# One plain column pair fewer and one more by Strassen's scheme in four feed-forward layers, with the activation sums asked for twice as densely

## The chip, the cores and the metric

The kernel runs on one core of one Trainium2 chip. The metric is the device time of one execution in microseconds (us), lower is better. A difference under 0.2% is about what a measurement of this kernel can't tell from none.

## What is computed

The reference is two transformer blocks one after the other, on 512 tokens of width 1024, in float32. The first has two layers, each with a feed-forward layer ("ffn1"), a mixer of three branches, and a second feed-forward layer ("ffn2"); the second has a mixer of four branches and a feed-forward layer with a convolution. The four feed-forward layers of the first block are those of this change:

```python
def swiglu(x, w_gu, w_down):
    gate, up = jnp.split(x @ w_gu, 2, axis=-1)
    return (jax.nn.silu(gate) * up) @ w_down
...
    h = layer_norm(DEEPNORM_ALPHA * x + 0.5 * swiglu(x, ffn1_w_gu, ffn1_w_down), ln_g[0], ln_b[0])
    ...
    return layer_norm(DEEPNORM_ALPHA * h + 0.5 * swiglu(h, ffn2_w_gu, ffn2_w_down), ln_g[2], ln_b[2])
```

`w_gu` is 1024 x 5632. Its first 2816 columns make the gate, the others what is multiplied by it: 22 column tiles of 128 each (FT = 22). A gate tile with the tile of the same number of the other half is a column pair, so each of the four layers has 22 pairs.

## The kernel before, in words

**Numbers.** Every float32 operand of a large product is split in a rounded high part and a rest ("hi" and "lo", type fp32r), and a product is hi*hi + hi*lo + lo*hi: three matmuls. Activations lie transposed, 128 features by 512 tokens to a page.

**Plain products.** `product` makes one column tile, 128 x 512: 8 blocks of 128 x 128 weights, 3 matmuls of 512 columns each (`block_matmuls`, L2490, L2491, L2499). Four blocks in the order of use make a slab of weights, 128 x 512, 256 KB. A slab is loaded by SyncE (`load_slab`, L3806), rounded by ScalarE (`round_slab`, L2813) and its rest is made by VectorE (`rest_slab`, L3235); the first matmul of the slab waits for that rest. There are 14 raw buffers and 9 for rounded parts. How far ahead the steps of a slab stand in each engine's queue is set by `place`, which is called once a block:

```python
        if j == 0:
            self.loaded(min(s - 1 + LOADED, self.limit - 1))
            self.rested(s)
        if j == 1:
            self.rounded(min(s + AHEAD, self.limit - 1))
        if j == 3:
            self.rested(min(s + AHEAD - 1, self.limit - 1))
```

With AHEAD = 4, the rest of slab s + 3 is put on VectorE's queue at the last block of slab s. The limit is the end of the plain products at the head.

**Pairs by Strassen's scheme.** A pair can also be made by 7 products of half size (`paired`, `pair_product`): each is 4 blocks of 3 matmuls with 256 columns (`pair_matmuls`, L2525, L2527, L2528), 84 matmuls in all. They come in the order q1, q5, q4 of the pair before, q6, q3, q2, q7. For a pair the weights have to be combined first (`prepare`, run step by step): 5 loads by SyncE (L3810), two of them added to by accumulating DMAs that GpSimd issues (L3799), two sums on VectorE (L3241 `sum_second`, L3247 `sum_fourth`), rounding on ScalarE (L2824 for one unit, L2822 for two), and rests on VectorE (L3256 for one unit, L3253 for two). q1 needs the rest of the single unit, q5 the first wide rest, q6 the second. The activations have to be combined too, once a layer: `sums_of` makes for each of 4 page pairs four half-page differences on VectorE (L3264, L3265, L3268, L3271; called T here), two rounded parts on ScalarE (L2829, L2832) and two rests on VectorE (L3277 twice; called S here). It is a generator that gives way between its parts:

```python
            self.sums_made(k, self.R[kt].f, self.R[4 + kt].f, self.Rt[kt], self.Rt[4 + kt], a, b)
            self.Rt[kt] = self.Rt[4 + kt] = k["t4"]
            for _ in range(4):
                yield
            k.will(scalar="ha hb", vector="la lb")
            self.sums_split(k, scale, a, b, ha, hb)
```

with four more `yield` at the end, so a page pair takes 8 steps and all take 32, and a 33rd ends it.

**The head of such a layer** (`ffn`). The first ALONE = 6 pairs are made plain. In three layers the first three pairs are made while the normalised activations come in (`Pace.begin`); in the first layer, which starts the kernel, it is two. Then one pair after the other is made by the loop in `ffn`: ahead of each column tile `taken_in` takes one finished pair in if there is one (ScalarE silu L2925, VectorE product L3454, ScalarE rounding L2928, VectorE rest L3457), and then 9 rounds per tile (8 blocks, and one that ends it) each emit a block and `self.bg.steps(1)`, one step of the sums. In the last plain pair the rounds also call `head.step(until=6)`: the six first steps of `prepare` for the first pair by Strassen's scheme. Each engine's instructions stand in its queue in the order in which Python calls them. `Pace` has a model of time that orders the background work in the mixers; in this loop it plays no part, as the sums alone are in its queue.

After the head come the pairs ALONE to FIRST - 1 by Strassen's scheme, then the first part of the down projection over FIRST = 11 tiles, then the other 11 pairs by Strassen's scheme, and the rest of the down projection.

Of the kernel before, what the change touches and what calls it, by code (L numbers as in the profile page):

```python
# [30 lines left out]
T5_MAX_DIST = 128  # L31

SLAB = 4
NSLAB = 1120 - 4 * 64
NPAIR = 64
NRAW = 14
NHI = 9
LOADED = 7
# [6 lines left out]
CONST_PARTS = 4  # L45
NGAIN = 48
UNIT = SLAB * P
ALONE = 6
FIRST = 11
QUARTERS = ("a11", "a21", "a22", "a12")  # L50

# [432 lines left out]
class Order:  # L484
# [29 lines left out]
    def __init__(self, memory):  # L514
# [8 lines left out]
        self.pair_order = []  # L523
        self.slab, self.multiplied, self.limit = {}, 0, NSLAB
        self.next_block = self.next_raw = self.next_round = self.next_rest = 0
# [19 lines left out]
    def until(self, blocks):  # L545

        self.limit = min(-(-(self.next_block + blocks) // SLAB), NSLAB)

    def loaded(self, s):
        while self.next_raw <= min(s, NSLAB - 1):  # L550
            unit = self.raws.take()
            self.slab[self.next_raw] = [unit, None]
            self.landing(unit)
            self.load_slab(self.next_raw, unit)
            self.next_raw += 1

    def rounded(self, s):
        while self.next_round <= min(s, NSLAB - 1):
            self.loaded(self.next_round)
            raw, hi = self.slab[self.next_round] = [self.slab[self.next_round][0], self.his.take()]  # L560
            self.round_slab(self.next_round, raw, hi)
            self.next_round += 1

    def rested(self, s):
        while self.next_rest <= min(s, NSLAB - 1):
            self.rounded(self.next_rest)
            self.rest_slab(self.next_rest, *self.slab[self.next_rest])
            self.next_rest += 1
# [494 lines left out]
    def ffn(self, source, X, up, down, scale, early, after, scaled=None, mem=None):  # L1063
        H = Operand(FIRST)
        pairs = [m for j in range(ALONE) for m in (j, FT + j)]
        self.until(len(pairs) * DT)
        if early:
            first = self.bg.got(self.bg.begin(source, X, [early.product(up, m) for m in pairs[:2]],
                                              [self.product(up, m, X) for m in pairs[2:6]], early.made))
        else:  # L1070
            first = self.bg.got(self.bg.begin(source, X, [], [self.product(up, m, X) for m in pairs[:4]], lead=2))
        open_pairs = [first[i:i + 2] for i in range(0, len(first), 2)]

        def taken_in():
            gate, lift = open_pairs.pop(0)
            s = self.pages.take()
            k = self.marks("ffn").will(scalar="silu", vector="times")
            h, l = self.pages.take(), self.pages.take()
            k.will(scalar="round", vector="rest")
            self.ffn_act(k, gate, lift, s, h, l)  # L1080
            self.banks.give(gate, k["silu"])
            self.banks.give(lift, k["times"])
            H.join((h, l, k["rest"]))
            self.pages.give(s, k["rest"])

        if scaled:
            self.bg.get(scaled)
        sums = self.bg.add(self.sums_of(X, 1.0 / ALPHA))
        head = self.pair(up, ALONE, FT + ALONE)
        for m in range(len(open_pairs), ALONE):  # L1090
            made = []
            for n in (m, FT + m):
                if open_pairs:
                    taken_in()
                w = Later(self.product(up, n, X))
                while not w.done:
                    self.bg.tell(w)
                    self.bg.steps(1)
                    if m == ALONE - 1 and not w.done and (n > FT or self.next_block % DT in (2, 5)):
                        head.step(until=6)  # L1100
                made.append(w.value)
            open_pairs.append(made)
        self.bg.get(sums)
        while open_pairs:
            taken_in()

        def ahead(blocks):
            self.until(blocks)
            s = self.next_block // SLAB
            self.loaded(s + 1)  # L1110
            yield
            self.loaded(s + 2)
# [3 lines that stand above are left out]
            self.loaded(s + 3)  # L1116
            self.rested(s + 1)
            yield
            self.loaded(s + 4)
            self.rested(s + 2)  # L1120

        head.step(until=6)
        follow = Later(self.product(down, 0, H))
        self.paired(up, range(ALONE, FIRST), X, H, head, ahead(FIRST * DT), follow)
        part, H = H, Operand(FT - FIRST)
        head = self.pair(up, FIRST, FT + FIRST)
        left = FIRST * DT
        for m in range(DT):
            w = Later(self.product(down, m, part)) if m else follow
            while not w.done:  # L1130
                self.bg.tell(w)
                left -= 1
                if left in (24, 20, 12, 9, 6, 3):
                    head.step()
            k = self.marks("norm").will(vector="sum")
            self.add_up(k, w.value, m, scale)
            self.Rt[m] = k["sum"]
            self.banks.give(w.value, k["sum"])
        self.drop(part, w.value.full)
        follow = Later(self.product(down, 0, H, k0=FIRST))  # L1140
        self.paired(up, range(FIRST, FT), X, H, head, ahead(NSLAB * SLAB), follow)
        self.drop(X, (self.lanes["pair"].tensor, self.lanes["pair"].raised[0]))
        return self.update(down, H, scale, Spread(self, after, after.count == 2), k0=FIRST, beside=mem, begun=follow)
# [900 lines left out]
    def run(self):  # L2044
# [7 lines left out]
        assert SLAB * (NSLAB - 1) < self.next_block <= SLAB * NSLAB, self.next_block  # L2052
        assert len(self.pair_order) == NPAIR, len(self.pair_order)

# [1922 lines left out]
```

## Time and profile before

| | us |
|---|---|
| median of 3 runs | 3561.03 |
| lowest and highest | 3560.19, 3562.94 |
| the profiled execution: span from first to last instruction | 3557.1 |
| TensorE busy with matmuls | 3502.0 |
| VectorE busy | 2226.9 |
| ScalarE busy | 1679.6 |

The median is 3.9 us over the span of the profiled execution, which is what lies around the span. Busy times of TensorE count overlapping, pipelined matmuls once, and their ends are modelled, so starts are what to go by: the time from one matmul's start to the next one's. An idle time in brackets stands ahead of the instruction that ended it, with what it had waited for.

### The profile page before, as it was taken

How to read it: one execution, taken by the hardware profiler on the slowest of the kernel's cores; microseconds unless marked ns; L12 is line 12 of the kernel's file. 1: busy time of each engine (PE TensorE's matmuls, PEld its weight loads, DVE VectorE, ACT ScalarE, POOL GpSimd, SP SyncE). 2: the span in 40 equal slices, each digit the busy share in tenths (PEclk: the TensorE clock that was granted, in tenths of full speed). 3: DMA queues.
4: the chain of work that ended last, by engine and by line, in shares of the span. 5: the costliest groups of instructions: out<-in, count | busy, mean ns of one | idle time of the engine just before them, and what ended most of it. 6: DMA issues, size and time to landing. Idle time of an engine off the chain costs nothing.

```text
span 3557.1 us, 49763 instructions
## 1 busy us (share of the span) xinstructions
PE 3502.0 (98%) x19256; PEld 2932.2 (82%) x19256; DVE 2226.9 (63%) x4229; ACT 1679.6 (47%) x3243; POOL 111.3 (3%) x132
## 2 busy tenths in 40 slices
PE   9999999999999999999999999999999999999999
PEld 7898878877888987998888877888977677788887
DVE  5566656556775667566665566765676786666643
ACT  5354455554353545454555543553455443444432
POOL 0010000000000100010000000001000000000000
PEclk9999999999999999999999999999999999999999
DMA  5474331112335743574221112255522222233332
GB/s 154 131 175 143 116 95 48 45 47 72 90 105 138 173 122 98 140 172 125 83 66 47 47 60 91 93 134 151 152 79 86 69 66 84 77 94 93 95 95 86
DMA packets 198276, 358.86 MB, mean 101 GB/s; under 512 B 22102, under 2 KB 26359, under 8 KB 198040
## 3 DMA queue, kind: packets, MB, share of 16 engines
q1 hardware_dynamic: 178840, 321.32, 29.8%
q0 software_dynamic: 18432, 33.56, 5.6%
q8 instruction: 153, 2.51, 0.3%
q10 hardware_dynamic: 768, 0.79, 0.1%
q14 instruction: 83, 0.68, 0.1%
HBM read 350.60 MB, written 4.72 MB: 100 GB/s over the span
## 4 chain that ended last, share of the span: by engine, by line
PE 93%; DVE 4%; ACT 2%; issue 1%; DMA 0%; DVEq 0%; ACTq 0%
PE bank L2490 21%; PE bank L2499 21%; PE bank L2491 21%; PE bank L2525 6%; PE bank L2527 6%; PE bank L2528 6%; PE bank L2478 2%; PE bank L2473 1%; PE bank L2568 1%; PE bank L2661 1%; PE bank L2671 1%; PE bank L2536 1%; PE bank L2759 1%; PE bank L2588 1%; DVE w_lo L3235 0%
## 5 line engine op out<-in xcount | busy, mean ns | idle before, releaser
L2490 PE MATMUL bank<-page_r,w_hi 128*128 128x512 f32 (+1 forms) x3446 | 1383.4, 401 | 21.9 <-DVE w_lo L3235 14.7
L2499 PE MATMUL bank<-page_r,w_lo 128*128 128x512 f32 (+1 forms) x3446 | 1359.7, 395 | 0.0
L2491 PE MATMUL bank<-page_r,w_hi 128*128 128x512 f32 (+1 forms) x3446 | 1349.8, 392 | 0.0
L2490 PEld LDWEIGHTS bank<-page_r,w_hi 128*128 128x128 f32 x3446 | 650.0, 189 | 182.5 <-DVE w_lo L3235 18.8
L2813 ACT ACTIVATE w_hi<-raw 128x512 fp32r<-128x512 f32 x864 | 532.8, 626 | 558.3 <-PE bank L2499 550.1
L2499 PEld LDWEIGHTS bank<-page_r,w_lo 128*128 128x128 f32 x3446 | 649.2, 188 | 145.7
L2491 PEld LDWEIGHTS bank<-page_r,w_hi 128*128 128x128 f32 x3446 | 649.9, 189 | 141.6 <-issue 3.6
L3235 DVE TENSOR_TENSOR w_lo<-raw,w_hi 128x512 fp32r<-128x512 f32 x864 | 574.9, 686 | 150.2 <-ACT w_hi L2813 149.8
L2525 PE MATMUL bank<-page_r,w_hi 128*128 128x256 f32 x1792 | 503.7, 281 | 2.5 <-DVE w_lo L3253 2.5
L2528 PE MATMUL bank<-page_r,w_lo 128*128 128x256 f32 x1792 | 503.4, 281 | 0.0
L2527 PE MATMUL bank<-page_r,w_hi 128*128 128x256 f32 x1792 | 503.4, 281 | 0.0
L2525 PEld LDWEIGHTS bank<-page_r,w_hi 128*128 128x128 f32 x1792 | 337.7, 188 | 3.9 <-ACT page_f L2842 3.2
L2527 PEld LDWEIGHTS bank<-page_r,w_hi 128*128 128x128 f32 x1792 | 337.6, 188 | 0.7
L2528 PEld LDWEIGHTS bank<-page_r,w_lo 128*128 128x128 f32 x1792 | 337.7, 188 | 0.0
L3325 DVE SCALAR_TENSOR_TENSOR page_f<-bank,page_f 128x512 f32<-128x512 f32 x96 | 66.3, 691 | 261.6 <-PE bank L2499 260.6
L3253 DVE TENSOR_TENSOR w_lo<-raw,w_hi 128x1024 fp32r<-128x1024 f32 x192 | 228.8, 1220 | 0.0
L2822 ACT ACTIVATE w_hi<-raw 128x1024 fp32r<-128x1024 f32 x192 | 202.2, 1056 | 43.0 <-DVE raw L3247 21.3
L3799 POOL DMA_DIRECT2D raw<-pairs x128 | 111.1, 892 | 2425.4 <-DMA raw<-pairs 2424.0
L2842 ACT ACTIVATE page_f<-bank 128x256 f32<-128x256 f32 x128 | 49.2, 384 | 208.5 <-PE bank L2528 208.5
L2885 ACT ACTIVATE page_f<-page_f 128x512 f32<-128x512 f32 (+1 forms) x81 | 48.4, 604 | 130.8 <-DVE page_f L3325 112.6
L3776 DVE SCALAR_TENSOR_TENSOR page_f<-bank,par,page_f 128x511 f32<-128x511 f32 x88 | 65.5, 749 | 60.7 <-ACT page_f L3195 59.1
L2982 ACT ACTIVATE page_f<-bank 128x256 f32<-128x256 f32 (+3 forms) x129 | 45.4, 392 | 104.8 <-PE bank L2478 104.5
(322 smaller groups left out, 3462.9 us busy)
## 6 DMA issues: line engine op xcount, KB each, us to landing
raw<-weights SPq DMA_DIRECT2D x864, 256.0 KB, 2.7
raw<-pairs SPq DMA_DIRECT2D x320, 256.0 KB, 3.3
raw<-pairs POOLq DMA_DIRECT2D x128, 256.0 KB, 5.8
page_f<-x_t SPq DMA_DIRECT2D x8, 256.0 KB, 5.2
bias_rows<-page_f SPq DMA_DIRECT2D x8, 256.0 KB, 2.0
page_f<-bias_rows SPq DMA_DIRECT2D x8, 256.0 KB, 3.9
out_t<-page_f SPq DMA_DIRECT2D x12, 128.0 KB, 1.8
cst<-consts SPq DMA_DIRECT2D x4, 272.0 KB, 3.5
```

What stands on the lines that cost most here:

```text
L2478: last = self.e.transpose(b.tile(i), ap[:, i * P:(i + 1) * P], self.const("ident"))
L2490: self.e.matmul(o, hi, X.hi[kt], start=first, stop=False)
L2491: self.e.matmul(o, hi, X.lo[kt], start=False, stop=False)
L2499: last = self.e.matmul(o, lo, X.hi[kt], start=False, stop=final)
L2525: self.e.matmul(b.cols(256), hi.r[:, c], x_hi, start=first and kt == 0, stop=False, skip_group_check=not first)
L2527: self.e.matmul(b.cols(256), hi.r[:, c], x_lo, start=False, stop=False, skip_group_check=not first)
L2528: last = self.e.matmul(b.cols(256), lo.r[:, c], x_hi, start=False, stop=kt == 3, skip_group_check=not first)
L2813: self.e.activation(hi.r, raw.f, ACT.Copy).then_inc(self.m.s_hi, 1)
L2822: self.e.activation(dst[0].wide_rounded(), src[0].wide(), ACT.Copy).then_inc(p.prep.lane.scalar, 1)
L3235: self.e.tensor_tensor(raw.r, raw.f, hi.r.bitcast(F32), ALU.subtract).then_inc(self.m.s_lo, 1)
L3253: self.e.tensor_tensor(src[0].wide_rounded(), src[0].wide(), hi[0].wide_rounded().bitcast(F32), ALU.subtract).then_inc(p.prep.lane.vector, 1)
L3799: self.e.dma_start(unit.f, self.m.pairs[p.number, QUARTERS.index(part)], accum_op=ALU.add) \
```

## The change

There is one plain pair fewer at the head of each of the four layers, and one more by Strassen's scheme ahead of the first part of the down projection (6 in place of 5 there, 17 in place of 16 in a layer, 68 in place of 64 in all). The weights of the four pairs move from the slabs to the array of pair weights. In the loop of the head two steps of the sums are taken in each round instead of one.

```diff
--- before.py
+++ after.py
@@ -31,8 +31,8 @@
 T5_MAX_DIST = 128
 
 SLAB = 4
-NSLAB = 1120 - 4 * 64
-NPAIR = 64
+NSLAB = 1120 - 4 * 68
+NPAIR = 68
 NRAW = 14
 NHI = 9
 LOADED = 7
@@ -45,7 +45,7 @@
 CONST_PARTS = 4
 NGAIN = 48
 UNIT = SLAB * P
-ALONE = 6
+ALONE = 5
 FIRST = 11
 QUARTERS = ("a11", "a21", "a22", "a12")
 
@@ -1095,7 +1095,7 @@
                 w = Later(self.product(up, n, X))
                 while not w.done:
                     self.bg.tell(w)
-                    self.bg.steps(1)
+                    self.bg.steps(2)
                     if m == ALONE - 1 and not w.done and (n > FT or self.next_block % DT in (2, 5)):
                         head.step(until=6)
                 made.append(w.value)
```

## Rows read from the trace of the kernel before

**Rows 1.** The page: busy times of TensorE, and the chain that ended last, by engine.

```profile
PE 3502.0 (98%) x19256; PEld 2932.2 (82%) x19256; DVE 2226.9 (63%) x4229; ACT 1679.6 (47%) x3243; POOL 111.3 (3%) x132
PE 93%; DVE 4%; ACT 2%; issue 1%; DMA 0%; DVEq 0%; ACTq 0%
```

**Rows 2.** Windows: stretch, length, PE, PEld, DVE, ACT, POOL busy (count), PEclk, DMA share, GB/s.

```profile
1171.15:1279.06 107.91, 107.91 (x913) 107.90 (x912) 79.51 (x117) 61.75 (x108) 15.62 (x18) 1.00 0.70 174
1112.36:1171.15 58.79, 58.79 (x254) 47.34 (x253) 20.07 (x31) 14.87 (x22) 3.48 (x4) 1.00 0.44 116
```

**Rows 3.** Timeline of TensorE at the head of the second layer: start, length, line.

```profile
1024.10 0.40 PE L2490 MATMUL bank<-page_r,w_hi 128*128 128x512 f32 x1
...
1044.19 0.50 PE L2490 MATMUL bank<-page_r,w_hi 128*128 128x512 f32 x1 [0.33 <-DVE w_lo L3235]
...
1058.99 0.28 PE L2525 MATMUL bank<-page_r,w_hi 128*128 128x256 f32 x1
...
1062.62 0.36 PE L2525 MATMUL bank<-page_r,w_hi 128*128 128x256 f32 x1 [0.63 <-DVE w_lo L3253]
```

**Rows 4.** Timeline of VectorE at the head of the second layer.

```profile
1026.61 0.69 DVE L3454 TENSOR_TENSOR page_f<-page_f,bank 128x512 f32<-128x512 f32 x1 [1.21 <-ACT page_f L2925]
...
1028.61 0.42 DVE L3264 TENSOR_TENSOR page_f<-page_f 128x256 f32<-128x256 f32 x1
...
1030.08 0.68 DVE L3235 TENSOR_TENSOR w_lo<-raw,w_hi 128x512 fp32r<-128x512 f32 x1
1030.68 1.28 DVE L3277 SCALAR_TENSOR_TENSOR page_r<-page_f,page_r 128x512 fp32r<-128x512 f32 x2
...
1039.82 0.68 DVE L3454 TENSOR_TENSOR page_f<-page_f,bank 128x512 f32<-128x512 f32 x1
...
1042.24 1.29 DVE L3277 SCALAR_TENSOR_TENSOR page_r<-page_f,page_r 128x512 fp32r<-128x512 f32 x2 [0.35 <-ACT page_r L2829]
1043.45 0.69 DVE L3235 TENSOR_TENSOR w_lo<-raw,w_hi 128x512 fp32r<-128x512 f32 x1
...
1053.55 0.69 DVE L3241 TENSOR_TENSOR raw<-raw 128x512 f32<-128x512 f32 x1
...
1055.36 1.22 DVE L3253 TENSOR_TENSOR w_lo<-raw,w_hi 128x1024 fp32r<-128x1024 f32 x1
1059.26 0.69 DVE L3454 TENSOR_TENSOR page_f<-page_f,bank 128x512 f32<-128x512 f32 x1 [2.69 <-PE bank L2499]
```

**Rows 5.** Timeline of ScalarE at the head of the second layer.

```profile
1030.19 0.63 ACT L2832 ACTIVATE page_r<-page_f 128x512 fp32r<-128x512 f32 x1 [0.16 <-DVE page_f L3271]
...
1055.47 1.06 ACT L2822 ACTIVATE w_hi<-raw 128x1024 fp32r<-128x1024 f32 x1 [1.69 <-DVE raw L3247]
1056.44 0.58 ACT L2925 ACTIVATE page_f<-bank 128x512 f32<-128x512 f32 x1
```

**Rows 6.** Timeline of TensorE at the head of the first layer.

```profile
29.71 0.40 PE L2490 MATMUL bank<-page_r,w_hi 128*128 128x512 f32 x1
...
75.30 0.28 PE L2525 MATMUL bank<-page_r,w_hi 128*128 128x256 f32 x1
...
78.93 0.36 PE L2525 MATMUL bank<-page_r,w_hi 128*128 128x256 f32 x1 [0.64 <-DVE w_lo L3253]
```

**Rows 7.** Timeline of VectorE at the head of the first layer.

```profile
32.42 0.69 DVE L3454 TENSOR_TENSOR page_f<-page_f,bank 128x512 f32<-128x512 f32 x1 [6.75 <-ACT page_f L2925]
```

**Rows 8.** Timeline of TensorE after two long idle times.

```profile
310.41 1.22 PE L2536 MATMUL bank<-page_f,cst 128*128 128x256 f32 x2 [3.36 <-DVE page_f L3355]
...
549.09 0.50 PE L2490 MATMUL bank<-page_r,w_hi 128*128 128x512 f32 x1 [2.22 <-DVE w_lo L3235]
```

**Rows 9.** Windows behind the same two idle times, columns as in rows 2.

```profile
310.40:316.80 6.40, 6.39 (x16) 5.11 (x17) 3.94 (x10) 4.08 (x10) 0.00 (x0) 0.54 0.15 41
...
549.00:554.00 5.00, 4.91 (x32) 4.41 (x33) 2.75 (x9) 0.60 (x1) 0.00 (x0) 1.00 0.00 0
```

**Rows 10.** DMA issues of the pair weights: count, KB each, median us to landing.

```profile
raw<-pairs SPq DMA_DIRECT2D x320, 256.0 KB, 3.3
raw<-pairs POOLq DMA_DIRECT2D x128, 256.0 KB, 5.8
```

## The prediction

> **What bounds the kernel now.** The page comes first: TensorE is busy for 98% of the span and makes up 93% of the chain that ended last [rows 1]. So time goes down only if TensorE gets less work, and goes up by every wait that it is given. The windows then give its two rates at the full clock: 912 matmuls of 256 columns start within 107.91 us, 118.3 ns each, and 252 of 512 columns within 58.79 us, 233.3 ns each [rows 2]. Last come the heads of the four layers, where the change acts. At the second layer's head TensorE waits for rests of slabs that VectorE makes (0.33 us at 1044.19, and a like wait later) and for a wide rest of the first pair by Strassen's scheme (0.63 us) [rows 3]. The page's 63% for VectorE hides this: from the first `taken_in` at 1026.61 on it hardly stops before 1056.6, and only then waits 2.69 us for TensorE [rows 4]. At this place VectorE is nearly the bound. The third and fourth layer show the same pattern to 0.1 us; one stands for three.
>
> **The work that is swapped.** Removed per layer: 48 matmuls of 512 columns, 48 x 233.3 ns = 11.20 us. Added: 84 of 256 columns, 84 x 118.3 ns = 9.94 us [rows 2]. TensorE gains 1.26 us a layer, 5.0 us in all. That is only 0.14% of the time.
>
> The Trainium skill (TensorE: Matmul & The Clock Gate, section Back-to-back issue gap) speaks against the swap: it gives for sustained streams of weight loads and matmuls about 131 ns at 512 columns and 81 ns at 128. By it a plain pair would be 48 x 131 ns = 6.3 us, one by Strassen's scheme at least 84 x 81 ns = 6.8 us, and my sum would be at least 7 us higher. The trace disagrees, with 233.3 and 118.3 ns.
>
> Other parts of the added pair: VectorE and ScalarE do more for it than for a plain one, but in the stretch of 912 matmuls (10.9 pairs) VectorE is busy for 79.51 us of 107.91, and ScalarE for 61.75 [rows 2]; TensorE covers both, and I cost them at nothing between 0 and 0.3 us a layer (the two sides of what steady pairs show). SyncE issues 5 loads for 4, GpSimd 2 adding DMAs; landing takes 3.3 and 5.8 us [rows 10]. The head pair's steps keep their distance from the end of the plain pairs, so its DMAs do too; cost nothing. If that cover were gone, a late load would cost its landing, 3.3 us, once a layer.
>
> **The sums, denser.** With one step a round they take 32 of the 48 rounds of blocks in the last three plain pairs, and the first pair's preparation has the last pair to itself. With two steps they take all but one of 18 rounds of one plain pair, and the preparation follows in the only pair left. VectorE's own work shrinks by four slab rests (0.60 us each) and one `taken_in` (2.0), 4.4 us, while TensorE's cover shrinks by 11.2. So I walk VectorE's new queue in the second layer, in the times of before up to 1026.61, when the chain starts. Lengths, from one start to the next [rows 4]: `taken_in` 2.0 (1026.61 to 1028.61, ScalarE's rounding in the middle of it); T 1.47; a slab's rest R 0.60, ready 0.69 after its start, and TensorE 0.05 later; S 1.2, but its second half has to wait for ScalarE's rounding of T's last part, which starts 1.58 after T and takes 0.63 [rows 4, 5]. Where S follows T at once it ends 2.87 after T's start (1.58 + 0.63 + 0.06 + 0.60). After a `taken_in` S starts 2.42 after the latter's start (1039.82 to 1042.24) and takes 1.21 [rows 4].
>
> The new order, by the rounds (T0 to T3 and S0 to S3 are the four page pairs' parts, R257 is the rest of slab 257): taken_in, T0, S0, R257, T1, S1, R258, T2, taken_in, S2, R259, T3, S3, R260, taken_in, R261, taken_in, then the first pair's sum, its rest, its second sum, its wide rest. Slab 257 is the fourth from the one that starts at 1024.10. TensorE wants a new slab every 2.80 us, so 257 at 1032.50.
> - T0 1028.61, S0 to 1031.48, R257 ready 1032.17: in time.
> - T1 1032.08, S1 to 1034.95, R258 ready 1035.64, wanted 1035.30: wait 0.4.
> - T2 1035.55, taken_in 1037.02, S2 1039.44, R259 starts 1040.65, TensorE goes on at 1041.39 and not at 1038.5: wait 2.9. Before, R259 stood right behind that taken_in.
> - T3 1041.25, S3 to 1044.12, R260 lets TensorE go at 1044.86, not 1044.19: wait 0.7.
> - taken_in 1044.72, R261 in time, taken_in 1047.32, sum 1049.32, rest 49.92, second sum 50.52, wide rest 51.12 to 52.34 (0.60 each and 1.22 [rows 4]). q1 is wanted at 1050.46: waits 0.2; q5 0.3.
> - ScalarE's second wide rounding waits for the second sum (0.72 after its start), silu follows 0.97 later and takes 0.6 [rows 5]; so the last taken_in starts at 1052.82, and from it to q6 it is 3.36 us, as from 1059.26 to 1062.62 [rows 3, 4]. q6 starts at 1056.18.
>
> Before, q6 started at 1062.62. Without any wait it would be there 1060.54 (1024.10 + 48 blocks of 0.70 + 24 x 0.1183), so 2.1 us were lost; after, 1024.10 + 22.40 + 2.84 = 1049.34, so 6.8 us are lost. Net for the layer: 4.7 - 1.26 = +3.5 us (check: 1056.18 - 1062.62 + 9.94 = +3.5). From q6 on VectorE has about 2.6 us to spare a pair ((107.91 - 79.51) / 10.9) and the order is the old one: nothing more is lost or won. Three layers: +10.5 us.
>
> The first layer makes only two pairs ahead of the sums, so a plain pair lies between them and the preparation. Its chain starts at 32.42 [rows 7], 994.19 us before that of the second layer, and the slab that the loop starts with at 29.71 [rows 6], 0.2 us earlier against the chain than there (1024.10 - 994.19 = 29.91). The same walk gives waits of 0.6, 2.9 and 0.7 us, then VectorE catches up in the plain pair between, and the last wait stays as it is, 0.8 (0.64 idle and a slower start). Lost after: 5.0; before: 78.93 - (29.71 + 44.80 + 2.84) = 1.6. Net 3.4 - 1.26 = +2.1 us.
>
> Sum: 10.5 + 2.1 = **+12.6 us**. Against the profiled execution, a span of 3557.1 becomes 3569.7; with the 3.9 us around it, that is 3573.6, on the median of 3561.0. The walk rests on starts of single rows and may be wrong by 0.7 us a layer, +-3 us in all. The mixers' order comes from a planner whose clock is shifted; a tie that falls otherwise there may move an instruction, below or above nothing, which I bound by one of the small waits seen, some 2 us either way.
>
> **Rivals.**
> - A, the forecast: VectorE becomes the bound at all four heads: 3573.6. For it: the chain before has no slack between 1026.61 and 1056.6, and its order and lengths are in the rows. Chance 0.75.
> - B, the other side: VectorE keeps up. A slab's rest stands on VectorE's queue up to three slabs ahead of its use. If VectorE ran through the denser queue that much ahead of TensorE, as its start is not bound to TensorE's blocks, the waits of the heads would stay at 2.1 and 1.6 us, and the 5.0 us are kept: 3556.0. Point from which it decides: the chain would have to start some 5 us earlier than 1026.61. Against it: the start is set by the silu ahead of it, which the change doesn't touch [rows 4]. Chance 0.04. Halfway (waits half as long, 3565) 0.06, which counts as no change.
> - C, the clock: idle time of 3.36 us was followed by a stretch with a granted clock of 0.54, mostly the 1.2 GHz level, for 6.4 us; after 2.22 us idle it stayed at 1.00 [rows 8, 9]. The new wait of 2.9 us lies between. A slow stretch gives away about 3 us. In the first layer 0.7 of it is absorbed in the next wait: +2.3. In the others VectorE is the bound there and hides it, unless the wait before q6 (2.4 us, behind 0.2 and 0.3) drops the clock, then up to 3 us each: 3576 to 3585, likeliest 3577. Chance 0.12. The Trainium skill (same page, section HAM oscillation) says of bursts with long idle gaps between that each gap throws the array back to the half clock; row 310.41 agrees, row 549.09 shows a gap that didn't.
> - D, the change doesn't do it so: the preparation of the first pair comes too late for its DMAs, q1 waits for a landing, 3.3 us a layer: 3587. Against: only the plan's distance to the plain pairs' end counts, and it is kept. Chance 0.03.
>
> **Numbers.** Likeliest is A, 3573.6. The range takes in A with its errors (3 and 2 us) and some more towards the halfway case, and on the other side C's likeliest: 3567 to 3579. Under 0.2% (7.1 us) either way is no change for a measurement. Slower by more takes 3568.2: A but for its low tail of 0.02, C and D: 0.88. Same: the halfway case, that tail, and half of B: 0.10. Faster takes 3553.9, which even the full 5.0 us don't reach; the other half of B, should the mixers come out ahead too: 0.02.
>
> **What would show it.** Right: at the second layer's head idle times of TensorE of about 0.3, 2.7 and 0.5 us ended by L3235, the large one where S2 stands ahead of the slab rest, and one of 2.2 us ended by L3253 ahead of q6; T and S of all four page pairs within 16 us; no 2.69 us wait of VectorE's last `taken_in` for TensorE. In the first layer the 2.7 us but not the 2.2. Wrong: idle times there as before (B), a granted clock under 1.00 behind them (C), waits of L3241 or L3253 for a DMA (D), or a difference outside the heads.

## The result and the profile after

The changed kernel takes 3577.62 us (median of 5 runs, 3577.24 to 3579.97) against 3561.03 (median of 5, 3559.11 to 3563.54). The ratio is 1.0051, with a 95% interval of 1.0038 to 1.0063: slower. The profiled execution has a span of 3575.4 us, 18.3 more than that of before. All differences by stage below are differences of these two spans.

The page of the kernel after, its busy times and its chain, against [rows 1]:

```profile
PE 3504.3 (98%) x19400; PEld 2940.2 (82%) x19400; DVE 2243.0 (63%) x4249; ACT 1691.0 (47%) x3259; POOL 118.5 (3%) x140
...
PE 91%; DVE 5%; ACT 3%; issue 1%; DMA 0%; SPq 0%; DVEq 0%; ACTq 0%
```

TensorE is busy for 2.3 us more, where it has 5.0 us less to do, and its share of the chain falls by two points. Both the waits and slow matmuls are in this. The waits of TensorE, first in the kernel before and then after (columns: total us, times, longest):

```profile
PE bank L2490 <- DVE w_lo L3235: 14.7, 11, 5.6
...
PE bank L2525 <- DVE w_lo L3253: 2.5, 4, 0.6
```

```profile
PE bank L2490 <- DVE w_lo L3235: 24.8, 15, 5.5
PE bank L2525 <- DVE w_lo L3253: 6.9, 4, 2.1
```

Slab rests cost TensorE 10.1 us more and the wide rests 4.4 more. No other line of that list differs by more than 0.5 us, and the three that differ by 0.3 to 0.5 lie outside the heads. The places are those of the prediction. TensorE at the head of the second layer, after (start, length, line, idle time ahead and what ended it), against [rows 3]:

```profile
1039.20 0.47 PE L2490 MATMUL bank<-page_r,w_hi 128*128 128x512 f32 x1 [0.30 <-DVE w_lo L3235]
...
1044.81 0.50 PE L2490 MATMUL bank<-page_r,w_hi 128*128 128x512 f32 x1 [2.58 <-DVE w_lo L3235]
...
1048.36 0.47 PE L2490 MATMUL bank<-page_r,w_hi 128*128 128x512 f32 x1 [0.49 <-DVE w_lo L3235]
...
1059.57 0.36 PE L2525 MATMUL bank<-page_r,w_hi 128*128 128x256 f32 x1 [2.07 <-DVE w_lo L3253]
...
1060.67 0.41 PE L2528 MATMUL bank<-page_r,w_lo 128*128 128x256 f32 x1
1060.88 0.41 PE L2525 MATMUL bank<-page_r,w_hi 128*128 128x256 f32 x1
```

The fourth wait stands before q6. The last two lines show what the forecast had not: their starts are 0.21 us apart, where steady ones are 0.118 apart. VectorE in the same stretch, against [rows 4]:

```profile
1030.06 0.69 DVE L3454 TENSOR_TENSOR page_f<-page_f,bank 128x512 f32<-128x512 f32 x1 [1.21 <-ACT page_f L2925]
...
1033.52 1.48 DVE L3277 SCALAR_TENSOR_TENSOR page_r<-page_f,page_r 128x512 fp32r<-128x512 f32 x2
...
1040.44 0.68 DVE L3454 TENSOR_TENSOR page_f<-page_f,bank 128x512 f32<-128x512 f32 x1
1041.82 0.69 DVE L3457 TENSOR_TENSOR page_r<-page_f,page_r 128x512 fp32r<-128x512 f32 x1 [0.70 <-ACT page_r L2928]
...
1042.86 1.29 DVE L3277 SCALAR_TENSOR_TENSOR page_r<-page_f,page_r 128x512 fp32r<-128x512 f32 x2 [0.35 <-ACT page_r L2829]
1044.07 0.69 DVE L3235 TENSOR_TENSOR w_lo<-raw,w_hi 128x512 fp32r<-128x512 f32 x1
...
1056.21 0.69 DVE L3454 TENSOR_TENSOR page_f<-page_f,bank 128x512 f32<-128x512 f32 x1 [0.47 <-ACT page_f L2925]
```

The slab rest at 1044.07, for which TensorE waits 2.58 us, stands behind a `taken_in` (in which VectorE stands idle for 0.70 us until ScalarE has rounded) and behind S (0.35 more). "Standing" is used below for such idle time in the middle of a unit of work. VectorE's chain from the first `taken_in` to the last takes 26.15 us (1030.06 to 1056.21); the walk gave 26.21 (1026.61 to 1052.82). The 2.69 us in which VectorE waited for TensorE before its last `taken_in` are gone.

Windows of the kernel after, columns as in rows 2: the time around TensorE's wait before q6, the stretch behind it, the one after that, and the stretch around the long wait in the first layer:

```profile
1057.50:1059.50 2.00, 0.00 (x0) 0.00 (x0) 1.91 (x3) 1.58 (x4) 0.00 (x0) 1.00 0.41 106
1060.50:1063.80 3.30, 3.30 (x18) 3.30 (x17) 1.35 (x3) 1.85 (x3) 0.00 (x0) 0.50 0.68 237
1064.00:1070.00 6.00, 6.00 (x53) 6.00 (x52) 5.02 (x7) 3.31 (x6) 1.64 (x2) 1.00 0.68 115
...
46.70:50.10 3.40, 3.00 (x7) 2.42 (x8) 3.27 (x8) 1.75 (x3) 0.00 (x0) 0.50 0.00 0
```

Behind the idle time the granted clock is 0.50, the 1.2 GHz level. Such a stretch is called slow here; this one lasts 3.4 us. The same stands behind q6's wait in the third and fourth layer (from 1422.3 and 2347.3). TensorE is counted busy all the while: 18 matmuls of 256 columns in 3.3 us, where 53 fit in 6.0 behind it.

Where the 18.3 us went, layer by layer. "To the head's end" is the time from the end of the Strassen part before (or from the start) to the first matmul of the pairs by Strassen's scheme; "first Strassen part" is from there to the first matmul of the down projection; "the rest" is from the end of the fourth layer's first Strassen part to the last matmul.

| layer | to the head's end, before / after | first Strassen part, before / after | net | forecast |
|---|---|---|---|---|
| 1 | 75.30 / 68.15 | 49.15 / 59.14 | +2.8 | +2.1 |
| 2 | 934.54 / 926.85 | 49.14 / 62.40 | +5.6 | +3.5 |
| 3 | 307.96 / 299.67 | 49.14 / 62.42 | +5.0 | +3.5 |
| 4 | 870.27 / 862.03 | 49.14 / 62.39 | +5.0 | +3.5 |
| the rest | 1165.57 / 1165.51 | | -0.1 | 0 |

Nearly everything lies in the heads and in the pairs right behind them, and 5.7 us of it are not in the forecast.

### The profile page after: what moved, and what is told of

Same layout as the page of the kernel before. It is cut to its first block, busy times and chain, and to the rows that moved or that the text cites. A ratio compares the mean times of both kernels' runs of the same rounds, so it can differ in the third digit from the quotient of the medians.

```text
span 3575.4 us, 50105 instructions
## 1 busy us (share of the span) xinstructions
PE 3504.3 (98%) x19400; PEld 2940.2 (82%) x19400; DVE 2243.0 (63%) x4249; ACT 1691.0 (47%) x3259; POOL 118.5 (3%) x140
## 4 chain that ended last, share of the span: by engine, by line
PE 91%; DVE 5%; ACT 3%; issue 1%; DMA 0%; SPq 0%; DVEq 0%; ACTq 0%
PE bank L2490 20%; PE bank L2499 20%; PE bank L2491 20%; PE bank L2525 6%; PE bank L2528 6%; PE bank L2527 6%; PE bank L2478 2%; PE bank L2473 1%; PE bank L2568 1%; PE bank L2661 1%; PE bank L2671 1%; PE bank L2536 1%; PE bank L2588 1%; PE bank L2759 0%; DVE w_lo L3235 0%
## 5 line engine op out<-in xcount | busy, mean ns | idle before, releaser
L2490 PE MATMUL bank<-page_r,w_hi 128*128 128x512 f32 (+1 forms) x3382 | 1358.6, 402 | 32.9 <-DVE w_lo L3235 24.8
L2499 PE MATMUL bank<-page_r,w_lo 128*128 128x512 f32 (+1 forms) x3382 | 1334.6, 395 | 0.0
L2491 PE MATMUL bank<-page_r,w_hi 128*128 128x512 f32 (+1 forms) x3382 | 1324.9, 392 | 0.0
L2490 PEld LDWEIGHTS bank<-page_r,w_hi 128*128 128x128 f32 x3382 | 638.1, 189 | 191.8 <-DVE w_lo L3235 25.9
L2813 ACT ACTIVATE w_hi<-raw 128x512 fp32r<-128x512 f32 x848 | 522.9, 626 | 557.8 <-PE bank L2499 549.3
L2499 PEld LDWEIGHTS bank<-page_r,w_lo 128*128 128x128 f32 x3382 | 637.3, 188 | 143.1
L2491 PEld LDWEIGHTS bank<-page_r,w_hi 128*128 128x128 f32 x3382 | 638.0, 189 | 138.8 <-issue 3.6
L3235 DVE TENSOR_TENSOR w_lo<-raw,w_hi 128x512 fp32r<-128x512 f32 x848 | 563.8, 686 | 149.8 <-ACT w_hi L2813 149.4
L2525 PE MATMUL bank<-page_r,w_hi 128*128 128x256 f32 x1904 | 537.8, 282 | 7.0 <-DVE w_lo L3253 6.9
L2527 PE MATMUL bank<-page_r,w_hi 128*128 128x256 f32 x1904 | 537.1, 282 | 0.0
L2528 PE MATMUL bank<-page_r,w_lo 128*128 128x256 f32 x1904 | 537.1, 282 | 0.0
L2525 PEld LDWEIGHTS bank<-page_r,w_hi 128*128 128x128 f32 x1904 | 360.9, 190 | 9.8 <-ACT page_f L2842 7.5
L2527 PEld LDWEIGHTS bank<-page_r,w_hi 128*128 128x128 f32 x1904 | 361.0, 190 | 0.6
L2528 PEld LDWEIGHTS bank<-page_r,w_lo 128*128 128x128 f32 x1904 | 361.1, 190 | 0.0
L3253 DVE TENSOR_TENSOR w_lo<-raw,w_hi 128x1024 fp32r<-128x1024 f32 x204 | 242.9, 1219 | 0.0
L2822 ACT ACTIVATE w_hi<-raw 128x1024 fp32r<-128x1024 f32 x204 | 214.6, 1056 | 43.9 <-DVE raw L3247 18.8
L3799 POOL DMA_DIRECT2D raw<-pairs x136 | 118.3, 895 | 2436.5 <-DMA raw<-pairs 2434.1
L3256 DVE TENSOR_TENSOR w_lo<-raw,w_hi 128x512 fp32r<-128x512 f32 x68 | 47.0, 692 | 77.9 <-ACT w_hi L2824 77.9
```

What stands on the lines that cost most here:

```text
L2490: self.e.matmul(o, hi, X.hi[kt], start=first, stop=False)
L2491: self.e.matmul(o, hi, X.lo[kt], start=False, stop=False)
L2499: last = self.e.matmul(o, lo, X.hi[kt], start=False, stop=final)
L2525: self.e.matmul(b.cols(256), hi.r[:, c], x_hi, start=first and kt == 0, stop=False, skip_group_check=not first)
L2527: self.e.matmul(b.cols(256), hi.r[:, c], x_lo, start=False, stop=False, skip_group_check=not first)
L2528: last = self.e.matmul(b.cols(256), lo.r[:, c], x_hi, start=False, stop=kt == 3, skip_group_check=not first)
```

## The experiments

The theories, as the expectations name them: V, that VectorE's order makes the waits as walked; K, that the clock falls behind q6's wait and that this is what the forecast missed; S, that the dense sums are innocent and only the shorter head costs; S2, that only the dense sums cost and five plain pairs with one step are fine. Eight runs followed, in two sets of four. In the first, the kernel before had a median of 3560.95 us over 25 runs, in the second 3559.20 over 24. All ratios are to it.

**e1_dense_only: the denser steps alone.** Six plain pairs, as before, with two steps of the sums a round.

```diff
-ALONE = 5
+ALONE = 6
```

> Edit: the kernel before (six plain pairs) with two steps of the sums a round. Theory V (VectorE's queue order and length): in layers 2 to 4 the waits of the slab rests are those of the changed kernel, 0.3, 2.6 and 0.5 us, VectorE catches up in the plain pair that is left, and the wait ahead of q6 stays at 0.6 us; lost 4.6 us in place of 2.1 in each, and in the first layer 4.8 in place of 1.6. Sum +10.7 us on the kernel before: 3572. Rival S (the dense sums are innocent, only the shorter head costs): 3561, waits as before.

Measured: 3572.53 us, ratio 1.0030 (1.0020 to 1.0040), span 3569.7. TensorE at the second layer's head:

```profile
1046.58 0.50 PE L2490 MATMUL bank<-page_r,w_hi 128*128 128x512 f32 x1 [2.57 <-DVE w_lo L3235]
...
1070.63 0.36 PE L2525 MATMUL bank<-page_r,w_hi 128*128 128x256 f32 x1 [0.63 <-DVE w_lo L3253]
```

The waits of 0.30, 2.57 and 0.49 us are there, and the one before q6 is 0.63 as in the kernel before, since a whole plain pair lies between. The first Strassen part takes 49.14 us, unchanged. So the denser steps alone, with no pair added, cost 11.6 us by the medians, against 16.6 for the whole change: V holds, and S, which had the waits as before and 3561, falls. The added pair costs what was said, too: where no slow stretch and no wait but the old one falls in it, the part takes 59.08 us (the first layer of e3 and of e8), 9.94 more than 49.14.

**e2_five_only: the swap alone.** Five plain pairs, one step a round.

```diff
-                    self.bg.steps(2)
+                    self.bg.steps(1)
```

> Edit: the changed kernel with one step of the sums a round. Theory V: in layers 2 to 4 VectorE's work up to q6 is the same, so q6 comes at the same time, about 29.4 us after the first taken_in starts, whatever the order; the waits move: 0.3 us at one slab, some 3.5 us ahead of q1 (for the first pair's preparation), 0.3 at q5 and 2.3 at q6. In the first layer the sums fit in two pairs and nothing is added. Sum 3 x 3.3 - 1.2, and 1.6 us of slow clock in each of three layers: about 3574 to 3575. Rival S2 (the two steps are what costs, five plain pairs with one step are fine): 3556.

Measured: 3566.43 us, ratio 1.0013 (1.0004 to 1.0022): 8 us less than expected, and 11 less than with the denser steps. TensorE at the second layer's head, and the window behind its first wait:

```profile
1049.79 0.36 PE L2525 MATMUL bank<-page_r,w_hi 128*128 128x256 f32 x1 [2.89 <-DVE w_lo L3256]
...
1055.21 0.36 PE L2525 MATMUL bank<-page_r,w_hi 128*128 128x256 f32 x1 [0.82 <-DVE w_lo L3253]
```

```profile
1050.80:1054.10 3.30, 3.30 (x18) 3.30 (x16) 2.13 (x4) 2.55 (x5) 0.00 (x0) 0.50 0.00 0
```

No slab is late now. The last part of the sums stands ahead of the first pair's preparation, and q1 waits for it, 2.89 us. The clock falls behind that wait as well, but there TensorE runs slowly towards a q6 that VectorE hasn't ready anyway, so the slow stretch shrinks q6's wait to 0.82. I had expected q6 at the same distance from the chain's start whatever the order. It came 28.5 us behind it (1026.69 to 1055.21), 1.0 sooner than after the change (1030.06 to 1059.57). Nearly all of that is S, which here never stands: each takes 1.29 us, while after the change three of the four take 1.47 to 1.48 and the fourth stands 0.35 (from the first to the last `taken_in` it is 25.16 us, not 26.15). The denser steps save nothing. But S2, which had expected 3556, falls as well: the shorter head by itself costs 5.5 us by the medians, where the swap should have given 5.0.

**e3_fill: q6's wait filled.** The changed kernel with 16 matmuls more between q5 and q6 of the first pair, in the second to fourth layer. Their product goes to a spare bank and isn't used.

```diff
+                    self.pair_fill(k, spare, X, 16)
...
+        for _ in range(n):
+            last = self.e.matmul(b.cols(256), self.m.mean_rounded[:, :], X.hi[0][:, HALF[0]], start=True, stop=True)
```

> Edit: the changed kernel, with 16 more matmuls of 256 columns into an unused bank between q5 and q6 of the first pair by Strassen's scheme in layers 2 to 4, where TensorE stood idle for 2.07 us (their result is not used). Theory K (the idle time ahead of q6 drops the clock): q6 starts when it did, the idle time shrinks to some 0.2 us, the granted clock stays at 1.00 behind it, and each of three layers gets back 1.5 to 1.7 us: 3572.7, 4.9 us below the changed kernel. Rival (the slow stretch has another cause, or its time is lost anyway): 3577.6 or more.

Measured: 3573.52 us, ratio 1.0033 (1.0020 to 1.0045), span 3571.1. The kernel does more and is 4.1 us faster than the changed one by the medians (4.3 by spans; 4.9 had been expected). The intervals of the two ratios overlap a little (1.0038 to 1.0063 for the changed kernel), so the stages below carry more weight than the difference of the medians. TensorE, and the windows behind q6 and behind a wait in the first mixer:

```profile
1057.35 2.08 PE L2541 MATMUL bank<-page_r,mean_rounded 128*128 128x256 f32 x16
1059.58 0.35 PE L2530 MATMUL bank<-page_r,w_hi 128*128 128x256 f32 x1
```

```profile
1059.60:1064.00 4.40, 4.40 (x37) 4.40 (x38) 3.36 (x6) 2.27 (x4) 0.00 (x0) 1.00 0.76 239
552.30:555.60 3.30, 3.30 (x13) 2.84 (x12) 0.67 (x2) 0.00 (x0) 0.00 (x0) 0.50 0.00 0
```

q6 starts at 1059.58, as in the changed kernel (1059.57): VectorE's wide rest sets it. Behind it the clock is 1.00, and from q6 to the end of the part it takes 55.45 us, not 56.97. So one slow stretch in these matmuls costs 1.5 us, three 4.6: K holds. Less was gained in all since slow stretches turned up at 552.3, where the kernel before has none, and in the third layer's head behind the 2.57 us wait. This is also the one experiment that takes the fall away and leaves q6 at the time that VectorE sets. As the place of a slow stretch changes between executions (e8 below), it has to be counted and not only seen once: where the clock hadn't fallen earlier in the head, it fell behind q6's unfilled wait in four heads of four (three in the first profile, one in e8's), and in none of the two here (second and fourth layer).

**e4_reordered: the rest of a `taken_in` put later.** In the changed kernel VectorE's rest (L3457) comes four rounds behind its product, and the S of a page pair behind the T of the next.

```diff
+            if kt:
+                split(*unsplit.pop(0))
...
+                    if rounds == 4:
+                        rest()
```

> Edit: the changed kernel with the same instructions in another order at the heads: the rest of a taken_in is put on VectorE's queue four rounds later (for the last one behind the second wide rest, which q6 needs), and S of a page pair stands behind T of the next. Theory V: VectorE no longer stands still for ScalarE, its chain from the first taken_in to q6 shrinks from 29.5 us to some 24 to 25, the wait ahead of q6 from 2.07 to at most 0.8 us, and the clock doesn't fall: 3577.6 less 4.5 us and 1.6 us in each of three layers, less some 3 us in the first: about 3556. If the waits were not VectorE's standing still but its work or the weights' DMAs: 3570 or more.

Measured: 3567.02 us, ratio 1.0015 (1.0006 to 1.0024). It is 10.6 us faster than the changed kernel, but 11 slower than expected. VectorE in the second layer's head shows why:

```profile
1037.84 0.68 DVE L3476 TENSOR_TENSOR page_f<-page_f,bank 128x512 f32<-128x512 f32 x1
1040.26 1.29 DVE L3299 SCALAR_TENSOR_TENSOR page_r<-page_f,page_r 128x512 fp32r<-128x512 f32 x2 [1.74 <-ACT page_r L2851]
1041.47 0.69 DVE L3257 TENSOR_TENSOR w_lo<-raw,w_hi 128x512 fp32r<-128x512 f32 x1
```

VectorE doesn't stand for the rest any more, but now 1.74 us for the S behind it. On ScalarE's queue the rounding of the tile (which waits for the product at 1037.84) stood ahead of the roundings that this S needs. I had moved one engine's half of the exchange and not the other's. The slab rests still stood behind it: TensorE waited 0.74 and 2.11 us for them.

**e5_five_late: both halves put later.** Five plain pairs and one step a round. ScalarE's rounding of a tile comes five rounds behind its silu, VectorE's rest at the sixth round; the last tile's rest stands behind the second wide rest. The table of silu is loaded at the end of the early products.

```diff
+                    if rounds == 6:
+                        rest()
+                    self.bg.steps(1)
+                    if rounds == 5:
+                        rounded()
...
+                o.preload_silu()
```

> Edit: five plain pairs, one step of the sums a round, and VectorE kept from standing still at the heads: a taken_in's rounding is put on ScalarE's queue five rounds later and its rest on VectorE's queue six rounds later (the last one's rest behind the second wide rest, which q6 needs), and silu's table is loaded ahead of the first taken_in. Nothing is computed otherwise. Theory V: VectorE has 5.1 us of work for 5.6 us of TensorE's in each column tile, so slab rests come in time, q1 and q5 wait for nothing, q6 for at most 0.3 us; the swap's 5.0 us and the 7.9 us that the kernel before loses at its heads are won, less about 1: 3549. If the swap's gain or VectorE's standing still is not real: 3556 to 3566.

Measured: 3550.88 us, ratio 0.9974 (0.9964 to 0.9984), span 3550.6. The window of the second layer's head, from VectorE's first `taken_in` to the first Strassen matmul, and under it the window of nearly the same work in the changed kernel (from its first to its last `taken_in`):

```profile
1022.43:1043.42 20.99, 20.99 (x91) 16.90 (x90) 20.78 (x40) 12.72 (x22) 3.46 (x4) 1.00 0.66 150
```

```profile
1030.06:1056.21 26.15, 22.75 (x101) 17.45 (x101) 22.11 (x42) 13.93 (x23) 3.49 (x4) 1.00 0.45 108
```

VectorE is busy for 20.78 of 20.99 us here, for 22.11 of 26.15 there, and TensorE never stops. From the first tile's product to the last's it takes 22.03 us (1022.43 to 1044.46) instead of 26.15, for the same list of work (four rests of tiles, five slab rests, all T and S, the first pair's sums and rests). What had made VectorE the bound was not its work but its standing for ScalarE. One wait is left, 0.66 us before q6. It is ended by ScalarE, which copies q1's product into q6's bank (`pair_seed`) behind the roundings on its queue:

```profile
1047.08 0.38 PE L2547 MATMUL bank<-page_r,w_hi 128*128 128x256 f32 x1 [0.66 <-ACT bank L2859]
```

**e6_six_late: the same reordering on the kernel before.** Six plain pairs, one step; the edits of e5 otherwise.

> Edit: the same reordering on the kernel before (six plain pairs, one step a round). Theory V: its head waits of 7.9 us in all go but for about 1: 3554, and the kernel with five plain pairs in the same order is 5.0 us faster, 1.26 us a layer, as 48 matmuls of 512 columns and 84 of 256 are timed. If TensorE gains nothing by the swap, the two are equal.

Measured: 3551.43 us, ratio 0.9979 (0.9970 to 0.9988), span 3548.8. One idle time over 0.1 us is left at the heads and in the first Strassen parts, of 0.16 us in the second layer; each of these parts takes 48.45 us, in that layer 48.85. I had expected e5 to be ahead by 5.0 us; it is ahead by 0.5, and the intervals overlap. By stages (time to the head's end plus the first part) the swap gains 1.7 us in the first layer (121.67 against 123.36), where no wait is added. In the second and third it gains nothing (980.89 against 980.86, and 355.18 against 355.12): the 0.66 us before q6 takes half of the 1.26, and small differences ahead of the heads the rest. In the fourth e5 is 2.6 us longer (920.03 against 917.40): ahead of the head's end it takes 3.1 us more than e6 less a plain pair, and there its profile has two slow stretches, at 1818.3 and 2098.1, that e6's doesn't have. So at the one head where it adds no wait the swap is worth about what was forecast, but a wait of 0.7 us or one slow stretch is as large. These stages come from one execution each, e5's 1.5 us slower than its median and e6's 0.8 faster, so that by the profiles e5 is the slower of the two.

**e7_five_late_only: e5 without the early load of silu's table.**

```diff
-            if self.number is not None and self.number % 3:
-                o.preload_silu()
```

> Edit: e5 without the earlier load of silu's table. Theory V: VectorE's chain starts 1.3 us later in layers 2 to 4; with 0.5 us to spare in each of four column tiles it still keeps up but for 0.3 to 0.8 us a layer: 3550 to 3552. If it is the chain's start that matters more than its waits, as much slower as e5 is fast: 3555 or more.

Measured: 3553.70 us, ratio 0.9983 (0.9974 to 0.9992), 1.7 us over the 3550 to 3552 that had been expected. The wait before q6 is 1.76 us in place of 0.66:

```profile
1047.57 0.38 PE L2545 MATMUL bank<-page_r,w_hi 128*128 128x256 f32 x1 [1.76 <-ACT bank L2857]
```

The part takes 60.24 us, and in the third layer 61.76, with a slow stretch (1404.9) behind that wait: 1.52 us again. The early load is worth 2.8 us by the medians. Its executions spread over 9.4 us, more than those of any other kernel here, so I don't take that figure to be better than 2 us.

**e8_after_again: the changed kernel once more, unedited,** to see what repeats.

> The changed kernel once more, unedited, for a second profile. Theory K with chance: the idle times ahead of q6 and at the third slab are the same to 0.05 us, but the slow stretches behind them need not be: each of the four layers has at most one or two of 3.4 us, and they can stand at other layers than in the first profile, with the span 1.7 us shorter for each that is missing. If the clock fell by a fixed rule of the idle time alone, all stand where they stood.

Measured: 3576.97 us, ratio 1.0047 (1.0035 to 1.0060). The long slab wait is 2.57 us again, but in the second layer the clock falls behind this one, and then q6's wait is shorter and the clock holds behind it. TensorE, and the two windows:

```profile
1046.00 0.80 PE L2490 MATMUL bank<-page_r,w_hi 128*128 128x512 f32 x1 [2.57 <-DVE w_lo L3235]
1060.75 0.36 PE L2525 MATMUL bank<-page_r,w_hi 128*128 128x256 f32 x1 [1.93 <-DVE w_lo L3253]
```

```profile
1045.50:1048.90 3.40, 2.90 (x7) 2.32 (x8) 3.27 (x8) 1.75 (x3) 0.82 (x1) 0.50 0.46 121
1061.00:1065.00 4.00, 4.00 (x36) 4.00 (x36) 2.97 (x6) 2.27 (x4) 0.00 (x0) 1.00 0.76 252
```

The third layer does the same; the fourth is as in the first profile. Where the clock falls in the head, VectorE hides it: the time to the head's end is 927.38 against 926.85 (+0.5), and the first part 60.38 against 62.40 (-2.0). The span is 3574.1 us, 17.0 more than before: by layers +4.0, +4.1, +4.0 and +5.0, and nothing in the rest. Of the first layer's +4.0, 1.0 us is a later start of VectorE's chain (33.38 in place of 32.35). The waits belong to the program, the places of the slow stretches to the execution.

## Why the prediction was wrong by 4.0 us

It gave 3573.6, with 3567 to 3579; measured were 3577.62, and by the ratio and the median before (1.0051 x 3561.03) 3579.2. The direction, the place and the waits were right; the sum of A left out what the clock does behind the waits.

- **What bounds the kernel, and the swap.** Right. The added pair costs 9.94 us where nothing else falls into it (e3, e8). The two parts without any wait, 58.38 us in the first layer of e5 and 48.45 in e6, differ by 9.93. The Trainium skill's figure for a sustained stream (TensorE: Matmul & The Clock Gate, Back-to-back issue gap), about 131 ns at 512 columns, had spoken against the swap; it doesn't hold for these matmuls, which start 233.3 ns apart [rows 2]. The prediction counts the 118.3 ns at 256 columns against the page as well, but they don't contradict its 81 ns at 128.
- **VectorE's queue.** Right in order and size. Waits of 0.30, 2.58 and 0.49 us against about 0.3, 2.7 and 0.5 idle (0.4, 2.9 and 0.7 with the slower start); the chain 26.15 us against 26.21. Before q6 2.07 against 2.2. In the first layer 0.40, 2.64 and 0.63. What the prediction misread is why VectorE was so near to being the bound: it "hardly stops", it said of the stretch to 1056.6, and it took a `taken_in` as 2.0 us of work. VectorE is busy there for 25.63 us of 29.97. It stands 0.70 us in each of five `taken_in`, as in this row of the kernel before:

```profile
1041.20 0.69 DVE L3457 TENSOR_TENSOR page_r<-page_f,page_r 128x512 fp32r<-128x512 f32 x1 [0.70 <-ACT page_r L2928]
```

- **The first layer.** +2.8 us against +2.1: the clock fell behind the 2.64 us wait (window 46.70 above), the case that rival C had priced at +2.3 there. It cost 0.7.
- **The failed step.** The sum of A puts the clock behind the new waits at nothing, and leaves it to rival C: "in the others VectorE is the bound there and hides it, unless the wait before q6 (2.4 us, behind 0.2 and 0.3) drops the clock". That exception is what happened, in all three layers of the first profile. I took it to be unlikely, at 0.12 for all of C, as one row had kept its clock behind 2.22 us [rows 8, 9]. One row was no ground for that: behind the same wait of 2.2 us in the mixer, three of the ten profiles have a slow stretch (e2 at 549.0, e3 and e4 at 552.2). The price was also mis-sized. The 3 us came from the 6.4 us of rows 9; the stretches behind q6 last 3.4. In them matmuls of 256 columns start 213 ns apart (the two rows above, 0.21 us) for 118, so one costs 3.4 us x (1 - 118 / 213) = 1.5 us; e3 measured 1.52. The Trainium skill (TensorE: Matmul & The Clock Gate, Back-to-back issue gap) gives columns / 1.2 ns at the half clock, 213 ns for 256 columns, and the trace agrees. Three times 1.5 us, the first layer's 0.7 and some 0.5 us ahead of the second layer's head make the 5.7 that the span was out. In e8's execution the same program is out by 4.4 us, 1.9 (with the later start, 1.0), 0.6, 0.5 and 1.5 by layers: the size of this term, too, belongs to the execution.
- **The base.** I put 3.9 us around the span, which was a median less the span of another execution. Each execution timed later shows 1.8 us between its time and its span (3577.24 and 3575.4 for the profile of after). The 3.9 us are thus not what lies around the span: the execution profiled before was some 2 us faster than the median. So the miss is 5.7 us from span to span (3569.7 forecast, 3575.4 measured) and 4.0 us from median to median.
- **The planner's order in the mixers and the DMAs (D).** Nothing of size, as forecast: 0.1 us in the rest, no wait for a load at the heads. But the 0.5 us ahead of the second layer's head are of this kind. In the mixer there TensorE waits for a load of constants, which it doesn't in the kernel before:

```profile
308.75 0.50 PE L2490 MATMUL bank<-page_r,w_hi 128*128 128x512 f32 x1 [0.54 <-DMA cst<-consts]
```

The range went wrong for the same reason, by 0.2 us at its upper side by the ratio: it took in C's likeliest, 3577, but not the 3579 to 3585 above it. That 3577 lies so near to the measured median is luck: it is 3.4 us over A, 2.3 for the first layer and 1.1 for the other three, where the spans show 0.7 and 5.0.

What stays open: why the clock falls behind one wait and not behind another of the same length. e8 shows that it changes between executions of one program. Why e5 isn't 3 us or more ahead of e6 is accounted for only in part (q6's wait); the mixers' slow stretches vary by execution, and I did not take further profiles of the two. Putting the last silu ahead of the second wide rounding on ScalarE, to shorten e5's 0.66 us wait, wasn't tried.

## What to carry to other kernels

Before work on an in-order queue is made denser, count how long the engine would stand for another engine in the middle of each unit; here the standing, not the work, made VectorE the bound, and putting both halves of each exchange later (e5, e6) made the kernel 0.2 to 0.3% faster than before, where the denser steps had made it 0.3% slower (e1) and with the swap 0.5%. When a half is moved, look at the other engine's queue as well, as e4 moved only one and got a 1.74 us stand for it. Give every new idle time of TensorE a second price, the slow matmuls behind it, unless something else already bounds that stretch.

## What the runs showed of the hardware that I had not expected

The granted clock fell to 0.50 behind an idle time of 2.07 us, three times in one execution, while it had held behind 2.22 us in the kernel before. The same program, run again, had the fall behind another wait of the same head. The Trainium skill (TensorE: Matmul & The Clock Gate, HAM oscillation) says that gaps between bursts throw the array back to the half clock, and advises an order of work that leaves none. Without the gap, e3's clock held at that place, with 16 matmuls more and 4.1 us less. Of the single waits in these profiles, those of 1.76 us had a slow stretch behind them in one of three (e7), those of 2.2 us in the mixer in three of ten, those of 2.57 us in the second to fourth layer in four of twelve, and those of 2.89 us in three of three (e2). A slow stretch costs only what the next wait can't absorb: about 0.5 us in the second layer's head of e8, 1.5 behind q6 in the first profile.
